# Expert rows in rounds of 64 instead of 128 in a two-layer encoder kernel: paired 64-column matmuls, half-row transfers, and router logits from f16 parts

## The reference

```python
for l in range(DEPTH):                         # DEPTH = 2, x is 1024 tokens x 1024
    proj = x @ w_in[l] + b_in[l]               # attention, retention, HGRN2, memory attention, gates
    ...
    mixed = jnp.sum(gates * up, axis=2) @ w_out[l]
    x = _layer_norm(DEEPNORM_ALPHA * x + mixed, ln_g[l, 0], ln_b[l, 0])
    x = _layer_norm(DEEPNORM_ALPHA * x + grouped_moe(x, w_router, b_router, w_e_in[l], w_e_out[l]), ...)

def grouped_moe(x, w_router, b_router, w_e_in, w_e_out):      # 16 experts in 4 groups
    probs = softmax(xt @ w_router + b_router)
    # the group with the largest probability, and in it the two best of its 4 experts
    xs = xt[tok]                                # 2048 rows (2 per token), sorted by expert
    h = lax.ragged_dot(xs, w_e_in, group_sizes)               # 1024 -> 1024
    h_gate, h_up = jnp.split(h, 2, axis=-1)
    y = lax.ragged_dot(silu(h_gate) * h_up, w_e_out, group_sizes)   # 512 -> 1024
    y = y * weight                              # and each row is added to its token
```

## Time and profile before

| | us |
|---|---|
| median of 3 runs | 3074.41 (3069.76 to 3074.84) |
| the profiled execution's own time | 3063.31 |
| its span, first to last instruction | 3061.6 |
| PE busy | 2818.0 (92%) |
| DVE busy | 1541.6 (50%) |
| ACT busy | 1163.3 (38%) |
| POOL busy | 307.1 (10%) |
| mean granted TensorE clock | 0.956 of full |

### The profile page before, as it was taken

How to read it: one execution, slowest core, us unless ns; L and a number is a source line. 1 busy time by engine, 2 the same in 40 slices (tenths; PEclk the granted TensorE clock), 3 DMA queues, 4 the chain that set the end, 5 groups by cost and what they waited for, 6 DMA issues and landing times.

```text
span 3061.6 us, 47346 instructions
## 1 busy us (share of the span) xinstructions
PE 2818.0 (92%) x15748; PEld 1489.9 (49%) x15749; DVE 1541.6 (50%) x2477; ACT 1163.3 (38%) x1845; POOL 307.1 (10%) x240
## 2 busy tenths in 40 slices
PE   6999999999999699999579999999999995999994
PEld 4555554554444445454345555555544453454542
DVE  3244463343345567656633345634433455577665
ACT  3234413222232157655432443222222321576663
POOL 0000000000000023322310000000000000132323
PEclk9999999999999799999779999999999996999996
DMA  7200001111115389977622000111111253699974
GB/s 256 69 1 29 28 19 51 35 39 48 52 63 192 117 289 350 328 253 234 224 96 70 28 1 28 35 35 43 44 52 52 77 189 139 223 340 357 319 253 144
DMA packets 150902, 398.56 MB, mean 130 GB/s; under 512 B 13700, under 2 KB 58928, under 8 KB 149904
## 3 DMA queue, kind: packets, MB, share of 16 engines
q1 hardware_dynamic: 133104, 327.59, 29.4%
q0 software_dynamic: 14816, 54.12, 6.9%
q10 hardware_dynamic: 2816, 14.68, 1.3%
HBM read 343.91 MB, written 56.63 MB: 131 GB/s over the span
## 4 chain that ended last, share of the span: by engine, by line
PE 78%; DVE 6%; issue 5%; PEld 3%; DMA 2%; ACT 2%; DVEq 2%; SPq 0%; POOL 0%; PEldq 0%; ACTq 0%; POOLq 0%
PE PA L2013 15%; PE PA L1589 10%; PE PA L1590 10%; PE PA L1591 10%; PE PB L2032 8%; PE PC L1570 3%; PE PB L1591 3%; PE PB L1589 3%; PE PB L1590 3%; PE PD L1589 1%; PE PD L1591 1%; PE PD L1590 1%; PE PA L1687 1%; PEld PA L1589 1%; PEld PA L1591 1%
## 5 line engine op out<-in xcount | busy, mean ns | idle before, releaser
L2013 PE MATMUL PA<-XT,RA 128*128 128x512 f16 x2304 | 511.2, 382 | 9.7 <-DVE RA L1016 6.2
L1589 PE MATMUL PA<-XT,W 128*128 128x512 f16 x1216 | 461.9, 380 | 0.7 <-issue 0.7
L1590 PE MATMUL PA<-XT,W 128*128 128x512 f16 x1216 | 461.5, 380 | 0.0
L1591 PE MATMUL PA<-XT,W 128*128 128x512 f16 x1216 | 461.4, 379 | 0.0
L2013 PEld LDWEIGHTS PA<-XT,RA 128*128 128x128 f16 x2304 | 226.2, 98 | 277.3 <-issue 15.6
L1016 DVE SCALAR_TENSOR_TENSOR XT<-OT,XT 128x1024 f16<-128x1024 f32 x256 | 295.0, 1219 | 40.6 <-ACT XT L894 40.5
L1016 DVE SCALAR_TENSOR_TENSOR W<-W 128x512 f16<-128x512 f32 (+2 forms) x320 | 199.6, 661 | 163.5 <-ACT W L669 152.2
L819 ACT ACTIVATE WK<-PA,bT 128x512 f32<-128x512 f32 x128 | 87.9, 687 | 496.1 <-PE PA L1591 495.6
L2032 PE MATMUL PB<-W,WK 128*128 128x512 f16 x1152 | 260.8, 384 | 6.7 <-DVE W L1016 4.4
L894 ACT ACTIVATE XT<-OT 128x1024 f16<-128x1024 f32 x240 | 230.9, 1043 | 44.4 <-issue 40.9
L1243 DVE SCALAR_TENSOR_TENSOR MKV<-WK,PB 128x512 f32<-128x512 f32 x96 | 66.0, 687 | 338.9 <-PE PB L1591 338.9
(11 more groups left out here) (348 smaller groups left out, 4229.7 us busy)
## 6 DMA issues: line engine op xcount, KB each, us to landing
OT<-in_w_e_in_dram SPq DMA_DIRECT2D x256, 512.0 KB, 7.6
RA<-in_w_e_out_dram SPq DMA_DIRECT2D x128, 512.0 KB, 8.3
W<-in_w_in_dram SPq DMA_DIRECT2D x104, 512.0 KB, 4.6
W<-in_w_branch_dram SPq DMA_DIRECT2D x32, 256.0 KB, 4.8
W<-in_w_out_dram SPq DMA_DIRECT2D x16, 512.0 KB, 5.2
x_rows<-RC SPq DMA_DIRECT2D x16, 512.0 KB, 5.1
y_sum<-RC SPq DMA_DIRECT2D x16, 512.0 KB, 5.8
OT<-y_sum SPq DMA_DIRECT2D x16, 512.0 KB, 4.3
```

Of the source, the lines that this page charges most:

```text
L1589: mm(dst, lhs(0), rhs(0), start=first, stop=False)
L1590: mm(dst, lhs(0), rhs(1), start=False, stop=False)
L1591: return mm(dst, lhs(1), rhs(0), start=False, stop=last)
L2013: q = mm(PA[:, half, :], ROWS[:, a, k * P:(k + 1) * P], EIS[:, b, k, half * HALF:(half + 1) * HALF], start=k == 0 and a + b == 0, stop=k = ...
```

## The change

The tiles get `HT` = 64 rows. The stationary operand of a product is 64 columns wide, and two matmuls are issued one after the other, one that writes PSUM partitions 0 to 63 and one that writes 64 to 127, each with its own half of the output columns. Each of them still has 512 moving columns, so a round has as many product matmuls as before (48 and 24). A row of 1024 f32 lies as two half rows of 512 in 128 partitions (partition p and p + 64), so a gather or a scatter still has 128 packets, now of 2 KB; the elementwise work on rows has half as many columns, and the transposes are 4 and 2 instead of 8 and 4. The tables grow from 32 to 48 tiles. The weights, their conversion and its place in the order of the engines stay as they are: every expert is still converted once per layer, in the round ahead of its first tile (first weights) and in the round of its first tile (second weights).

The router's logits are made from f16 parts: ACT's copy becomes a high part, DVE makes a low part (`x1_low`, after its work on the next block), and PE does 24 f16 matmuls of 16 columns instead of 8 in f32.

```diff
-TILES = 2 * T // P + E
+HT = P // 2
+TILES = 2 * T // HT + E
...
-        ROW = RA[:, 4 * T:5 * T]
+        ROW = RA[:, 4 * T:4 * T + HALF]
-        YROW = WK[:, 2048:3072]
+        YROW = WK[:, 2048:2560]
+        half_rows = lambda a: a[:, :].rearrange("r (i n) -> (r i) n", i=2)
...
-                    nc.gpsimd.indirect_dma_start(ROW, None, x1_rows, bass.IndirectOffsetOnAxis(column, 0)
+                    nc.gpsimd.indirect_dma_start(ROW, None, half_rows(x1_rows), bass.IndirectOffsetOnAxis(column, 0)
...
-                        nc.scalar.copy(WK[:, 2048:3072], flat(PC)).then_inc(x1_cp, 1)
+                        nc.scalar.activation(X1S[:, 0, :, :], flat(PC).rearrange("p (k q) -> p k q", k=KD), ACT.Copy,
+                                             scale=SX).then_inc(x1_hi, 1)
...
-                    nc.scalar.activation(ROWS[:, 0, :], flat(PC), ACT.Copy, scale=SX).then_inc(row_hi, 1)
+                    nc.scalar.activation(ROWS[:, 0, :], PC[:, 0, :], ACT.Copy, scale=SX).then_inc(row_hi, 1)
...
-                    nc.scalar.activation(YROW, flat(PB), ACT.Copy, scale=row_wt[:, bass.ds(i, 1)]).then_inc(y_ev, 1)
+                    nc.scalar.activation(YROW, PB[:, 0, :], ACT.Copy, scale=row_wt[:, bass.ds(i, 1)]).then_inc(y_ev, 1)
...
+                def x1_low(t):
+                    v.wait_ge(x1_hi, at(x1_hi, t + 1))
+                    low_part(X1S[:, 1, :, :], flat(PC).rearrange("p (k q) -> p k q", k=KD), SX, X1S[:, 0, :, :]
+                             ).then_inc(x1_lo, 1)
...
-                    transposes(PC, ROW, 8).then_inc(row_tr, 1)
+                    transposes(PC, ROW, KD // 2).then_inc(row_tr, 1)
...
-                            for half in range(2):
-                                q = mm(PA[:, half, :], ROWS[:, a, k * P:(k + 1) * P],
-                                       EIS[:, b, k, half * HALF:(half + 1) * HALF],
+                            for i in range(2):
+                                q = mm(PA[i * HT:(i + 1) * HT, 0, :].rearrange("p (g n) -> p g n", g=2),
+                                       ROWS[:, a, k % KF * P + k // KF * HT:k % KF * P + (k // KF + 1) * HT],
+                                       EIS[:, b, k, :].rearrange("p (g i n) -> p i g n", g=2, i=2)[:, i, :, :],
                                        start=k == 0 and a + b == 0, stop=k == KD - 1 and a == 1)
...
-                            for half in range(2):
-                                q = mm(PB[:, half, :], HIDS[:, a, k * P:(k + 1) * P],
-                                       EOS[:, b, k, half * HALF:(half + 1) * HALF],
+                            for i in range(2):
+                                q = mm(PB[i * HT:(i + 1) * HT, 0, :],
+                                       HIDS[:, a, k % 2 * P + k // 2 * HT:k % 2 * P + (k // 2 + 1) * HT],
+                                       EOS[:, b, k, i * HALF:(i + 1) * HALF],
                                        start=k == 0 and a + b == 0, stop=k == KF - 1 and a == 1)
```

More of the change, by code:

```diff
@@ L2019, in transpose_hidden @@
                     pe.wait_ge(hid_ok, g0 + i + 1)
-                    for k in range(KF):
-                        q = nc.tensor.transpose(PD[:, 0, k * P:(k + 1) * P], WK[:, 512 + k * P:512 + (k + 1) * P], ident)
+                    for k in range(2):
+                        q = nc.tensor.transpose(PD[:, 0, k * P:(k + 1) * P], HID[:, k * P:(k + 1) * P], ident)
                     q.then_inc(hid_tr, 1)
```

86 lines of the change are left out of this document (53 added, 33 removed).

## The result

| | before | after |
|---|---|---|
| median, runs of one comparison | 3074.62 (3069.76 to 3077.09, 4 runs) | 3192.51 (3187.56 to 3201.64, 4 runs) |
| the profiled execution's own time | 3063.31 | 3187.56 |
| its span | 3061.6 | 3185.8 |

The changed kernel is slower by 3.9%: ratio 1.0393, 95% interval 1.0376 to 1.041. The profiled executions differ by 124.3 us. The prediction said 3208, +139 on the profiled execution.

A forecast was written before the change was run, and what follows sets the result against it. PE, busy 92% of the span, was taken as the bound. Stage +86 us per layer, twice, less 25 (ends) and 8 (router, tables) gave +139 on 3063.3: 3202, or 3213 in median terms; stated 3208, range 3110 to 3310.

The forecast's parts named there:

- Plain round 8.8: Experts' stage: a round without new weights takes PE 8.8 us instead of 16.85, pairs overlapping fully.
- First weights +5.0: Round splitting new first weights: 13.8 us instead of 8.8; T is the end of the last first product with old weights.
- Second weights +3.6: Round splitting second weights behind store and scatter landing: +3.6 us, the middle of +1.7 and +5.5.
- 8.6 per change: Each change of expert costs 8.6 us, bounds 6.7 and 10.5; 15 changes make 129 us per layer.
- The ends -25: Layers' first products (-5 each) and tails after the last silu (-9 and -6): together -25 us.
- Router and tables -8: Router logits -6 us and tables +2.7 a layer, net -4; -8 us for two layers.
- Rival 3: Scatter and gather bound each round, 6.4 to 10.2 us per scatter: 3275 us, up to 3340; chance 15%.
- Rival 2: Product pairs overlap only in part, 0.27 us a pair: about 3320 us; without overlap about 3550; chance 9%.
- Rival 4's floor: Weight transfers, 115 MB per layer at 283 GB/s, take 407 us, below the stage's 472; no separate chance given.
- The bound of +25 for a lower clock: PE idling lowers the granted clock; if half of the expert changes pay 1.7 us, +25 us.
- Rival 1: Weight conversion stays hidden and all rounds are plain: 2944 us; break-even at 4.0 us per change; chance 10%.

The follow-up runs named there:

- experiment 1: Changed kernel with every round using the first expert's weights, none loaded or split within the loop: 2952.52 us, ratio 0.9611 to the kernel before.
- experiment 2: Changed kernel with both matmuls of a pair writing to PSUM partitions 0 to 63, so they can't run side by side: 3573.77 us, ratio 1.1636.
- Experiments 3: Changed kernel with the second weights' splitting moved ahead of hidden_high and store_rows, on DVE ahead of hidden_low: 3134.41 us, ratio 1.0198 to the kernel before.
- experiment 4: Changed kernel, order kept, with GpSimd copying YROW to a second buffer for the scatter, so store_rows waits for the copy, not the landing: 3143.91 us, ratio 1.0246.
- experiment 11: Kernel before with only the router's f16 logits from the change: 3059.61 us, ratio 0.9965 to the kernel before.
- experiment 5: Changed kernel with second weights ahead of the store, plus table values for the next first weights read ahead of silu and hidden: 3068.6 us, ratio 0.999.
- experiment 7: Changed kernel with second weights ahead of the store and four first-weight chunks ahead of silu, in two orders: 3133.78 us (1.0186) and 3129.64 us (1.0192).
- experiment 10: Changed kernel with second weights ahead of the store, early table values and one first-weight chunk ahead of silu: 3055.98 us, ratio 0.9949 to the kernel before.
- experiment 6: Changed kernel with four of the eight first-weight chunks split ahead of silu: 3132.59 us, ratio 1.02 to the kernel before.
- experiment 9: Changed kernel with second weights ahead of the store, early table values and three first-weight chunks ahead of silu: 3086.11 us, ratio 1.0042 to the kernel before.

## Why the prediction was right

The time fell 15 us below the forecast and well within its range, and the mechanism is the one forecast. (The "about 4.5%" belongs to the sum's 3213; 3208 is 4.3% over 3074.4.) Two terms were off in opposite directions and in part cancel, the plain round and the change of expert. By its steps:

- **Plain round 8.8:** 8.97 in the trace after, and 8.97 in experiment 1. Pairs overlap in full; experiment 2 shows what they would cost otherwise. Forecast 0.17 too low per round, 7 us a layer.
- **First weights +5.0:** 5.2 (1.8 of waiting, 3.4 of DVE's pace), with the splitting at T + 3.1 where the prediction took 2.7.
- **Second weights +3.6:** the landing was put at T + 18.6 to 22.4 and is at 20.8; the scatter at 14.1 and is at 14.3. The round with second weights takes 12.3 us in the mean of layer 1 (11.9 to 12.9; 1190.92 to 1203.37 is one), +3.3 against 8.97. The forecast's +3.6 was the middle between two landings, a choice and not worked out, so that it came this close is partly luck. Experiments 3 and 4 show the cause as forecast: landing, store, then the splitting.
- **"8.6 per change": the term that was mis-sized.** (467.6 - 39 x 8.97) / 15 = 7.9 in layer 1, and 8.0 by experiment 1. The prediction said that costs add where an expert has two rounds. They don't wholly: the issue time behind the second weights and the wait for the next first weights are the same stretch, 1.76 us counted once (2.1 to 2.2 from the hidden transposes to the next product, in either case, against 0.37). That makes 12.45 + 12.38 - 2 x 8.97 = 6.9 for an expert of two rounds, and 8.6 for one of three. Too much by 0.7 x 15 = 11 us a layer; less the 7 from the plain rounds, the stage comes out at 467 where 472 was forecast, and 2 x 5 = 10 of the 15 us are here.
- **The ends -25:** the first products gave 5.9 and 5.6, the tails 11.2 and 7.9: -31. Nothing is split behind the last silu of layer 1, as forecast, and 7.6 us are left where the prediction took 10.
- **Router and tables -8:** outside the silus the two traces differ by 81.7 + 80.7 - 124.2 = 38 us; less 31 for the ends, 7 to 8 are left. In layer 1, from the transposes of the first block to the tables' first product are 92.5 us where they were 99.3, -6.8 as forecast (experiment 11 has -11 for both layers, with an interval of -16 to -6). From there to the experts' first product are 25.9 us where they were 24.7, so the tables cost 1.2 a layer and not the 2.7 forecast. That makes -11; the other 3 to 4 us come back somewhere else, and the cause stays open.
- **Rival 3 (scatter and gather bound each round)** falls with experiment 1, and in the changed kernel no plain round waits for rows. But where rounds are shorter or the store comes late they bind in some rounds (1.10 us of waiting for rows at 1227.81 in experiment 5, and the waits of experiment 7). **Rival 2** falls with the 0.221 of a pair. **Rival 4's floor** of 407 us per layer, at 283 GB/s, was no floor: experiment 10's stage has 396.
- **The bound of +25 for a lower clock** assumed that half of the changes pay 1.7 us. The clock did fall in 18 stretches, between the silus to 0.96 and 0.97 in the mean. Yet only four first products are longer by it, 1.7 us each, 7 us in all; elsewhere DVE's pace hides it.
- **Rival 1 (2944)** is what experiment 1 gives, 2953, if changes cost nothing. Its break-even of 4.0 us per change stands up well: experiment 5 still pays (404.9 - 350) / 15 = 3.7, and its time equals that of before within 0.2%.

## What to carry to other kernels

When a tile is halved, the work that is done once per weight keeps its size, and what must be compared with it is the stretch of PE's work between the last use of the old weights and the first of the new ones, not the busy share over the stage. Work that frees itself only when PE has passed a point should not stand in the queue behind a wait for something else, a landing or even three register reads; each of these was free while a round took 16.85 us, and cost 58 and 66 us when it took 9. Moving work ahead of the critical step helps only for as much as fits before that step: one chunk gained 13 us, three lost 17. And when a kernel is changed so that PE no longer waits for another engine, the granted clock must be looked at again: stretches at the lower level that cost nothing behind DVE's pace cost 1.4 to 2.7 us a product without it.

## What the runs showed of the hardware

- Two f16 matmuls with 64 stationary columns and 512 moving ones, one to output partitions 0 to 63 and one to 64 to 127, with different operands, run side by side: a new pair starts every 0.221 us, hardly more than one 128-column matmul alone (0.2155). Written to the same partitions they take 0.218 each.
- Reading a value from SBUF into a register takes 0.28 us on ACT's queue and 0.31 on PE's. Three of them with their register work and a branch delayed ACT by 1.84 us, two with the loop's branch PE by up to 2.3. The profile shows this as "issue".
- A GpSimd copy of 128 x 512 f32 took 0.60 us in the median of the 80 of experiment 4, and up to 1.62.
- The same 24 pairs that take 5.30 us at a granted clock of 1.00 took 6.99 at 0.76 (1419.55 in the changed kernel) and 7.94 at 0.66 (1201.11 in experiment 6). The clock fell after PE had idled: 1.10 and 1.76 us within one round in experiment 9 (1173.12), 4.04 and 1.80 in experiment 6. In experiment 10, with 0.99 us of idling in front of the new product at 1190.31, it stayed at 1.00.
